# Interleaving the weight blocks in pairs, and walking the moving tiles of the rounded products from the last token to the first

## The chip, the cores and the metric

The kernel runs on one core of a Trainium2 chip. The metric is the device time in microseconds (us) of one execution. The median of three runs of the kernel before is 1629.67 us (1629.29 to 1630.35).

## The reference

Two transformer-like blocks are applied to 512 tokens of width 1024, all in float32. The first block normalises, projects with `w_in`, runs three mixers (a gated delta rule, a sparse attention with a learned index, a convolution), projects back with `w_out`, adds a cross-attention to a memory of 256 tokens, and ends with a two-layer network of width 4096. The second block projects with a matrix to seven times the width (`w_in_2`), runs a gated convolution and a gated linear recurrence, merges the two through four more projections, and ends with a gated network of width 2816.

```python
x = x + jnp.square(jax.nn.relu(rms_norm(x, norm_mlp) @ mlp_w1)) @ mlp_w2      # first block, its end
proj = rmsnorm(x, ln1_g) @ w_in                                               # second block
merged = sigmoid(gate_a + bias_0) * (y_a @ w_out_a) + sigmoid(gate_b + bias_1) * (y_b @ w_out_b)
x = x + merged @ w_o
x = x + (silu(h @ w_ffn_gate) * (h @ w_ffn_up)) @ w_ffn_down
```

Nearly all arithmetic is in these dense products of 512 tokens with weight matrices.

## The kernel before

Activations lie turned: 128 features on the partitions, the 512 tokens along the row. A tile is 128 features by 512 tokens. Each weight matrix is cut on the host into blocks of 128 by 128 (`panels`), and up to eight blocks that feed one output tile lie side by side as a panel of 128 x 1024 values. The SyncE queue brings 276 panels in order through two buffers `raw` (`sync_program`).

A dense product is computed in three products of rounded values. Each panel is split once into `w_hi`, the value rounded to the chip's rounded 32-bit type, and `w_lo`, what is left: ScalarE writes `w_hi` (L1384 in most of the kernel) and VectorE `w_lo` (L1981), into four slots of 1024 columns each. Activations are split alike, into `h_hi` and `h_lo`, `u_hi` and `u_lo`, and so on. For each block, `products` (L622 to L628) issues three matmuls into one accumulator of TensorE's memory: `w_hi` with the high activations, `w_hi` with the low ones, `w_lo` with the high ones. The weight block is the stationary operand, which is loaded anew for every matmul (one LDWEIGHTS each), the activation tile is the moving operand. `panel` (L630) walks the blocks of a panel; it first waits until the panel is split, and at its end it gives the slot back (`s_panel_used`). The order of the panels and of the products is written out by hand in `tensor_program`: the projection of the first block, whose products stand between the small matmuls of the delta rule as filler (`front`, `FILL`), then the cross-attention, then loops (`Fori`) over the two halves of the first network (up, down), the seven projections of the second block (`mix_tile`, panels of 7 or 8 blocks by `MIX_CUTS`), the merge, `w_o`, the gated network and its down projection (panels of 6, 6, 5 and 5 blocks by `DOWN_CUTS`).

Where operands lie in a partition of the on-chip memory is set in `plan_memory`: buffers follow each other from an aligned base, and L203 puts the activations at a fixed remainder. `w_hi` and `w_lo` begin at bytes that are 128 modulo 512, the activation buffers of the large stages at 192 modulo 512, and the pair `ub_hi`, `ub_lo` of the recurrence at 416.

```python
    top[0] += (192 - top[0]) % 512
    h0 = top[0]
    k.h_hi, _ = sb("h_hi", KT * T, F32R)
```

A block of 128 columns is 512 bytes of a partition, a moving tile 2048 bytes, so these remainders are the same for all blocks and tiles of a buffer.

Some matmuls are of other kinds. L692 multiplies the memory's values with the operands exchanged: activations `m_hi` and `m_lo` are stationary there and the weight panel is moving. L764, L800 and others work on unrounded values.

Of the kernel before, what the change touches and what calls it, by code (L numbers as in the profile page):

```python
# [54 lines left out]
WT_BANKS, GO_BANKS = (6, 7, 1, 2), (2, 0, 2, 0)  # L55
PAIRS, BEAT = TT * HEADS, 3

F32 = mybir.dt.float32
# [429 lines left out]


def til(buf, j, n=1, w=T):  # L490

    return buf[:, j * w:(j + n) * w]
# [122 lines left out]
def tensor_program(nc, k):  # L615
# [7 lines left out]

    def products(out, w_at, wn, a_hi, a_lo, first, last):

        for n, (w, a) in enumerate(((k.w_hi, a_hi), (k.w_hi, a_lo), (k.w_lo, a_hi))):
            mm = e.matmul(out, w[:, w_at:w_at + wn], a, start=first and n == 0, stop=last and n == 2)  # L627
        return mm  # L628

    def panel(out, hi, lo, tiles, first=True, last=True, at=0, done=True, w=T, ready=None):  # L630

        slot = pan.slot().start
        if at == 0:

            e.wait_ge(k.s_split_done, RAW + pan.at(1))
        for n, t in enumerate(tiles):
            if ready:
                e.wait_ge(ready[0], ready[1] + t + 1)  # L640
            mm = products(out, slot + (at + n) * P, P, hi[:, t * w:(t + 1) * w], lo[:, t * w:(t + 1) * w],
                          first and n == 0, last and n == len(tiles) - 1)
        if done:
            mm.then_inc(k.s_panel_used, 1)
            pan.step()
        return mm
# [419 lines left out]
    for j in range(0, KT, 2):  # L1066

        width = 2 if j == 0 else 1
        for j0 in range(j, j + 2, width):
            outs = [acc.take(e, 4 + (j0 + n) % 2) for n in range(width)]  # L1070
            slots = []
            for n in range(width):
                e.wait_ge(k.s_split_done, RAW + pan.at(1))
                slots.append(pan.slot().start)
                pan.step()
            for t in range(KT):
                if t < HEADS:
# [62 lines left out]
    def wo_part(tiles, heads):  # L1140

        for n in tiles:
            if heads[0] == 0:
                acc.take(e, n)
                if n % 2 == 0:
                    e.wait_ge(k.s_split_done, RAW + pan.at(1))
                    wo_slots.append(pan.slot().start)
                    pan.step()
            for h in heads:
                e.wait_ge(k.s_ao_lo_done, h + 1)  # L1150
                mm = products(k.ps[n][:], wo_slots[n // 2] + (HEADS * (n % 2) + h) * P, P, til(k.ao_hi, h), til(k.ao_lo, h),
                              h == 0, h == HEADS - 1)
            if h == HEADS - 1:
                mm.then_inc((k.s_wo_first, k.s_panel_used)[n % 2], 1)
# [48 lines left out]
    for a, b in ((0, 4), (4, 6), (6, 7), (7, KT)):  # L1203

        for n in range(2):
            if a == 0:
                acc.take(e, n)
                e.wait_ge(k.s_split_done, RAW + pan.at(1))
                up_slots.append(pan.slot().start)
                pan.step()  # L1210
            for t in range(a, b):
                e.wait_ge(k.s_fed_lo, 3 * KT + t + 1)
                mm = products(k.ps[n][:], up_slots[n] + t * P, P, til(k.h_hi, t), til(k.h_lo, t), t == 0, t == KT - 1)
            if b == KT:
                mm.then_inc(k.s_panel_used, 1)
                if n == 0:
                    sum_squares(4 * KT, 3, k.sqacc)
    for j in range(2, 4):
        panel(acc.take(e, j)[:], k.h_hi, k.h_lo, range(KT))
    for half in range(2):  # L1220

        with e.Fori(0, MTH // 4 - (half == 0)) as i:
            pan.enter(i, 4)
            acc.enter(i, [2, 2, 0, 0, 0, 0, 0, 0])
            for j in range(4):
                panel(acc.take(e, j % 2)[:], k.h_hi, k.h_lo, range(KT))
            pan.leave(MTH // 4 - (half == 0))
            acc.leave(MTH // 4 - (half == 0))
        with e.Fori(0, KT // 2) as i:
            pan.enter(i, 4)  # L1230
            acc.enter(i, [1, 1, 0, 0, 0, 0, 0, 0])
            for j in range(2):
                out = acc.take(e, j)[:]
                ready = (k.s_up_lo, MTH * half)
                panel(out, k.u_hi, k.u_lo, range(0, 8), last=False, ready=ready)
                panel(out, k.u_hi, k.u_lo, range(8, 16), first=False, ready=ready)
            pan.leave(KT // 2)
            acc.leave(KT // 2)
# [7 lines left out]
    def mix_tile(u_lo, opening):  # L1246

        for a, b in zip(MIX_CUTS, MIX_CUTS[1:]):
# [6 lines left out]
            for n in order:  # L1255
# [23 lines left out]
    for n, (hi, lo) in enumerate(both):  # L1279
# [3 lines left out]
        for t in range(KT - 1):  # L1283
            e.wait_ge(k.s_s2_free, t + 1)
            products(out[:], slots[n] + t * P, P, til(hi, t), til(lo, t), t == 0, False)
        pan.step()
    e.wait_ge(k.s_s2_free, KT)
    for n, (hi, lo) in enumerate(both):
        t = KT - 1
        products(k.ps[n][:], slots[n] + t * P, P, til(hi, t), til(lo, t), False, True).then_inc(k.s_panel_used, 1)  # L1290
    for n, (hi, lo) in enumerate(both):
        panel(acc.take(e, 2 + n)[:], hi, lo, range(KT))
    with e.Fori(0, KT // 2 - 1) as i:
        pan.enter(i, 4)
        acc.enter(i, [1, 1, 1, 1, 0, 0, 0, 0])
        for j in range(2):
            for n, (hi, lo) in enumerate(both):
                panel(acc.take(e, 2 * j + n)[:], hi, lo, range(KT))
        pan.leave(KT // 2 - 1)
# [3 lines left out]
    with e.Fori(0, 2) as i:  # L1303
        pan.enter(i, 4)
        acc.enter(i, [2, 2, 0, 0, 0, 0, 0, 0])
        for j in range(4):
            panel(acc.take(e, j % 2)[:], k.mg_hi, k.mg_lo, range(KT), ready=(k.s_mg_lo, 0))
        pan.leave(2)
# [3 lines left out]
    for j in range(4):  # L1312
        panel(acc.take(e, j)[:], k.h_hi, k.h_lo, range(KT), ready=(k.s_fed_lo, 5 * KT))
        if j == 0:
            sum_squares(6 * KT, 5, k.sqacc)
    with e.Fori(0, FFN // 2 - 1) as i:
        pan.enter(i, 4)
        acc.enter(i, [1, 1, 1, 1, 0, 0, 0, 0])
        for j in range(4):
            panel(acc.take(e, j)[:], k.h_hi, k.h_lo, range(KT))  # L1320
# [1412 lines left out]


# [71 lines left out]
```

## Time and profile before

| | |
|---|---|
| median of three runs | 1629.67 us |
| the profiled execution, first to last instruction | 1626.4 us |
| TensorE matmuls busy | 1595.6 us (98%), 7524 matmuls |
| TensorE weight loads busy | 1311.0 us (81%), 7524 loads |
| VectorE busy | 912.4 us (56%) |
| ScalarE busy | 684.1 us (42%) |
| GpSimd busy | 157.1 us (10%) |
| DMA | 149.50 MB, mean 92 GB/s |
| mean granted TensorE clock | 0.997 of full |

The profile's page gives no time of the profiled execution other than this span; the rest of this document works on the span. Matmuls overlap each other in the trace: a record lasts from its start to the modelled arrival of its last result. What one matmul costs in a stream is therefore the distance from its start to the next start, not its duration. `acc` is any of the eight accumulators, and numbers of buffers and tiles are left out of all names.

### The profile page before, as it was taken

How to read it: one execution, taken by the hardware profiler on the slowest of the kernel's cores; microseconds unless marked ns; L12 is line 12 of the kernel's file. 1: busy time of each engine (PE TensorE's matmuls, PEld its weight loads, DVE VectorE, ACT ScalarE, POOL GpSimd, SP SyncE). 2: the span in 40 equal slices, each digit the busy share in tenths (PEclk: the TensorE clock that was granted, in tenths of full speed). 3: DMA queues.
4: the chain of work that ended last, by engine and by line, in shares of the span. 5: the costliest groups of instructions: out<-in, count | busy, mean ns of one | idle time of the engine just before them, and what ended most of it. 6: DMA issues, size and time to landing. Idle time of an engine off the chain costs nothing.

```text
span 1626.4 us, 21588 instructions
## 1 busy us (share of the span) xinstructions
PE 1595.6 (98%) x7524; PEld 1311.0 (81%) x7524; DVE 912.4 (56%) x1319; ACT 684.1 (42%) x996; POOL 157.1 (10%) x97
## 2 busy tenths in 40 slices
PE   6999999999999999999999999999999999999997
PEld 5888798788788888888888888888888888888886
DVE  4549799765664323444377666666455544444332
ACT  5735554554653213433244545554224434443221
POOL 3445486100000000000000000000000000000000
PEclk9999999999999999999999999999999999999999
DMA  7521100122123232233233333333322323222332
GB/s 286 165 78 65 52 1 2 65 86 96 40 91 103 91 103 90 90 104 103 59 105 106 93 93 93 93 93 104 104 90 91 104 90 102 91 93 86 99 97 77
DMA packets 45665, 149.50 MB, mean 92 GB/s; under 512 B 4784, under 2 KB 5936, under 8 KB 45616
## 3 DMA queue, kind: packets, MB, share of 16 engines
q1 hardware_dynamic: 42240, 139.90, 27.1%
q10 hardware_dynamic: 3376, 8.95, 1.5%
q8 instruction: 31, 0.51, 0.1%
q14 instruction: 18, 0.15, 0.0%
HBM read 146.47 MB, written 2.10 MB: 91 GB/s over the span
## 4 chain that ended last, share of the span: by engine, by line
PE 91%; DVE 6%; DMA 1%; ACT 1%; issue 0%; ACTq 0%; DVEq 0%; SPq 0%
PE acc L627 84%; DVE c_acc L2105 1%; DVE tok L2243 1%; DMA x<-xT 1%; DVE d_score_a L2246 1%; PE acc L938 1%; DVE d_score_b L2246 1%; PE acc L963 1%; PE acc L1113 0%; PE acc L1134 0%; DVE g_x L2229 0%; PE acc L800 0%; PE acc L702 0%; DVE w_lo L1973 0%; DVE x L2681 0%
## 5 line engine op out<-in xcount | busy, mean ns | idle before, releaser
L627 PE MATMUL acc<-h_hi,w_hi 128*128 128x512 f32 x1248 | 492.3, 394 | 1.4 <-issue 0.8
L627 PE MATMUL acc<-h_hi,w_lo 128*128 128x512 f32 x1248 | 491.6, 394 | 0.0
L627 PE MATMUL acc<-h_lo,w_hi 128*128 128x512 f32 x1248 | 488.7, 392 | 0.0
L1981 DVE TENSOR_TENSOR w_lo<-raw,w_hi 128x1024 fp32r<-128x1024 f32 (+2 forms) x241 | 281.5, 1171 | 81.7 <-ACT w_hi L1384 59.7
L1384 ACT ACTIVATE w_hi<-raw 128x1024 fp32r<-128x1024 f32 (+2 forms) x241 | 241.9, 1007 | 178.2 <-PE acc L627 86.4
L627 PEld LDWEIGHTS acc<-h_hi,w_hi 128*128 128x128 f32 x1248 | 234.8, 188 | 54.3 <-issue 3.8
L627 PEld LDWEIGHTS acc<-h_lo,w_hi 128*128 128x128 f32 x1248 | 234.9, 188 | 53.4 <-issue 1.0
L627 PEld LDWEIGHTS acc<-h_hi,w_lo 128*128 128x128 f32 x1248 | 234.9, 188 | 49.2
L627 PE MATMUL acc<-u_hi,w_hi 128*128 128x512 f32 x256 | 100.9, 394 | 0.0
L627 PE MATMUL acc<-u_hi,w_lo 128*128 128x512 f32 x256 | 100.4, 392 | 0.0
L2384 DVE TENSOR_TENSOR x<-x,acc 128x512 f32 x32 | 22.0, 688 | 139.2 <-PE acc L627 138.7
L627 PE MATMUL acc<-u_lo,w_hi 128*128 128x512 f32 x256 | 99.3, 388 | 0.0
L2651 DVE TENSOR_TENSOR f_t<-acc,rstd 128x512 f32<-128x512 f32 x44 | 30.4, 691 | 98.5 <-PE acc L627 98.3
L627 PE MATMUL acc<-f_hi,w_lo 128*128 128x512 f32 x176 | 69.3, 394 | 0.0
L627 PE MATMUL acc<-f_lo,w_hi 128*128 128x512 f32 x176 | 69.0, 392 | 0.0
L553 POOL TENSOR_TENSOR w_lo<-raw,w_hi 128x1024 fp32r<-128x1024 f32 x25 | 61.3, 2452 | 78.5 <-ACT w_hi L1377 78.2
L627 PE MATMUL acc<-f_hi,w_hi 128*128 128x512 f32 x176 | 68.3, 388 | 0.0
L1911 ACT ACTIVATE f_hi<-f_t 128x512 f32 x22 | 13.9, 632 | 116.5 <-DVE f_t L2657 116.5
L1825 ACT ACTIVATE u_t<-u_t 128x512 f32<-128x512 f32 x32 | 20.2, 632 | 93.9 <-DVEq L2526 88.8
L2523 DVE SCALAR_TENSOR_TENSOR u_t<-acc,rstd 128x512 f32<-128x512 f32 x28 | 19.4, 691 | 69.1 <-PE acc L627 69.1
L627 PEld LDWEIGHTS acc<-u_hi,w_lo 128*128 128x128 f32 x256 | 48.1, 188 | 11.3
L627 PEld LDWEIGHTS acc<-u_lo,w_hi 128*128 128x128 f32 x256 | 48.1, 188 | 10.8
(394 smaller groups left out, 2323.1 us busy)
## 6 DMA issues: line engine op xcount, KB each, us to landing
raw<-panels_a SPq DMA_DIRECT2D x112, 512.0 KB, 3.3
raw<-panels_b SPq DMA_DIRECT2D x68, 512.0 KB, 3.3
raw<-mix SPq DMA_DIRECT2D x48, 448.0 KB, 3.4
raw<-mix SPq DMA_DIRECT2D x16, 512.0 KB, 3.7
raw<-down SPq DMA_DIRECT2D x16, 384.0 KB, 3.2
raw<-down SPq DMA_DIRECT2D x16, 320.0 KB, 2.9
x<-xT ACTq DMA_DIRECT2D x4, 1024.0 KB, 9.5
x_rows<-xN ACTq DMA_DIRECT2D x2, 1024.0 KB, 8.6
```

The lines of the kernel that those rows point to most:

```text
L553: TTn(lo, raw, hi.bitcast(F32), ALU.subtract).then_inc(k.s_split_done, 1)
L627: mm = e.matmul(out, w[:, w_at:w_at + wn], a, start=first and n == 0, stop=last and n == 2)
L938: e.matmul(k.ps[4 + u % 2][:, 0:(qt + 1) * P], k.d_q[r, (h // 2) * T + qt * P:(h // 2) * T + (qt + 1) * P], k.d_k[r, 0:(qt + 1) * P], star ...
L963: mm = e.matmul(k.ps[(7, 3)[qt % 2]][:, h * 64:(h + 1) * 64], k.d_pt[:, (u % 2) * T + t * P:(u % 2) * T + (t + 1) * P], k.d_v[:, t * 64:(t ...
L1384: A(k.w_hi[:, ahead.slot(w)], k.raw[:, ahead.unsplit(w)], ACT.Copy).then_inc(k.s_weights_hi, 1)
L1825: A(k.u_t[:, (2 + j % 2) * T:(3 + j % 2) * T], k.u_t[:, (j % 2) * T:(j % 2 + 1) * T], ACT.Square).then_inc(k.s_up_sq, 1)
L1981: TTn(lo, raw, k.w_hi[:, ahead.slot(w)].bitcast(F32), ALU.subtract).then_inc(k.s_split_done, 1)
L2105: ins = STT(out=out, in0=y, scalar=w, in1=out, op0=ALU.mult, op1=ALU.add)
L2246: replaced[qt] = link(e.match_replace(scores[qt], tok(TOK_M8 + 8 * qt - 8, 8), scores[qt], TAKEN))
L2384: TTn(x, x, k.ps[b][:], ALU.add).then_inc(k.acc_free[b], 1)
L2523: STT(out=til(k.u_t, j % 2), in0=k.ps[j % 2][:], scalar=0.0, in1=k.rstd[:], op0=ALU.max, op1=ALU.mult).then_inc(k.acc_free[j % 2], 1)
L2651: TTn(til(k.f_t, j + 2 * n), k.ps[b][:], k.rstd[:], ALU.mult).then_inc(k.acc_free[b], 1)
```

## The change

A stage is given a pair `(n, turned)` in a table `ORDER`, and every stage has `(2, True)`.

The first value is about the weights. On the host, `ordered` takes the blocks of a panel two by two and interleaves their columns: column 0 of the first block, column 0 of the second, column 1 of the first, and so on. In the kernel `stationary` picks a block out again by a view of every second column, so that its 128 columns are 8 bytes apart and spread over 1024 bytes. Where a panel has an odd number of blocks, its last block stays as it was, with columns side by side. The panels of the memory's values (`wv`), whose weights are the moving operand, stay as they were.

The second value is about the moving tile. `turned_back` gives it with its columns in descending order, and the output in descending order too, so that each token's result lands where it did.

Number, size and order of the instructions, transfers, waits and buffers stay the same; the split of a panel works on all its columns as before.

```diff
--- before.py
+++ after.py
+ORDER = {"front": (2, True), "up0": (2, True), "dn0": (2, True), "up1": (2, True), "dn1": (2, True), "mix": (2, True), "merge": (2, True), "w_o": (2, True), "ffn": (2, True), "down": (2, True)}
...
+def stationary(w, slot, block, blocks, order):
+
+    n, _ = order
+    g = block // n * n
+    n = min(n, blocks - g)
+    a = slot + g * P + block - g
+    return w[:, a:a + (P - 1) * n + 1:n]
+
+
+def turned_back(ap, order):
+
+    return ap[:, ::-1] if order[1] else ap
...
-    def products(out, w_at, wn, a_hi, a_lo, first, last):
+    def products(out, slot, block, a_hi, a_lo, first, last, order, blocks=KT):
 
         for n, (w, a) in enumerate(((k.w_hi, a_hi), (k.w_hi, a_lo), (k.w_lo, a_hi))):
-            mm = e.matmul(out, w[:, w_at:w_at + wn], a, start=first and n == 0, stop=last and n == 2)
+            mm = e.matmul(turned_back(out, order), stationary(w, slot, block, blocks, order), turned_back(a, order), start=first and n == 0, stop=last and n == 2)
...
-    def panel(out, hi, lo, tiles, first=True, last=True, at=0, done=True, w=T, ready=None):
+    def panel(out, hi, lo, tiles, first=True, last=True, at=0, done=True, w=T, ready=None, order=ORDER["front"], blocks=KT):
...
-            mm = products(out, slot + (at + n) * P, P, hi[:, t * w:(t + 1) * w], lo[:, t * w:(t + 1) * w],
-                          first and n == 0, last and n == len(tiles) - 1)
+            mm = products(out, slot, at + n, hi[:, t * w:(t + 1) * w], lo[:, t * w:(t + 1) * w],
+                          first and n == 0, last and n == len(tiles) - 1, order, blocks)
...
-                    mm = products(out[:], slot + t * P, P, til(k.y_hi, t), til(k.y_lo, t), t == 0, t == KT - 1)
+                    mm = products(out[:], slot, t, til(k.y_hi, t), til(k.y_lo, t), t == 0, t == KT - 1, ORDER["front"])
...
-        panel(acc.take(e, j)[:], k.h_hi, k.h_lo, range(KT))
+        panel(acc.take(e, j)[:], k.h_hi, k.h_lo, range(KT), order=ORDER["up0"])
...
-                mm = products(out[:], slot + (n - a) * P, P, til(hi, t), til(lo, t), first, last)
+                mm = products(out[:], slot, n - a, til(hi, t), til(lo, t), first, last, ORDER["mix"], b - a)
...
-                      ready=(k.s_f_lo_done, 0))
+                      ready=(k.s_f_lo_done, 0), order=ORDER["down"], blocks=b - a)
...
+def ordered(p, order):
+
+    n, _ = order
+    out, blocks = [], p.shape[2] // P
+    for g in range(0, blocks, n):
+        b = p[:, :, g * P:min(g + n, blocks) * P].reshape(p.shape[0], P, -1, P)
+        out.append(b.transpose(0, 1, 3, 2).reshape(p.shape[0], P, -1))
+    return out[0] if len(out) == 1 else np_concatenate(out)
...
-    panels_a = cat([wk, wv, panels(w_in), panels(a["w_out"][0]), panels(a["xa_wq"][0]), wo,
-                    up[:MTH], dn[0], up[MTH:], dn[1]], 0)
+    fr = lambda p: ordered(p, ORDER["front"])
+    panels_a = cat([fr(wk), wv, fr(panels(w_in)), fr(panels(a["w_out"][0])), fr(panels(a["xa_wq"][0])), fr(wo),
+                    ordered(up[:MTH], ORDER["up0"]), ordered(dn[0], ORDER["dn0"]), ordered(up[MTH:], ORDER["up1"]),
+                    ordered(dn[1], ORDER["dn1"])], 0)
...
+    mix = cat([ordered(mix[:, :, s * P:t * P], ORDER["mix"]) for s, t in zip(MIX_CUTS, MIX_CUTS[1:])], 2)
...
-    panels_b = cat([merge, panels(a["w_o_2"][0]), ffn], 0)
+    panels_b = cat([ordered(merge, ORDER["merge"]), ordered(panels(a["w_o_2"][0]), ORDER["w_o"]), ordered(ffn, ORDER["ffn"])], 0)
...
+    down = cat([ordered(down[:, :, s * P:t * P], ORDER["down"]) for s, t in zip(DOWN_CUTS, DOWN_CUTS[1:])], 2)
...
```

Every other call of `products` and `panel` for rounded products gets its stage's `order` in the same way.

## Rows read from the trace of the kernel before

**Rows 1.** The page: busy time, share of the span and instructions of each engine.
```profile
PE 1595.6 (98%) x7524; PEld 1311.0 (81%) x7524; DVE 912.4 (56%) x1319; ACT 684.1 (42%) x996; POOL 157.1 (10%) x97
```

**Rows 2.** The page: the chain that ended last, by engine and by line.
```profile
PE 91%; DVE 6%; DMA 1%; ACT 1%; issue 0%; ACTq 0%; DVEq 0%; SPq 0%
PE acc L627 84%; DVE c_acc L2105 1%; DVE tok L2243 1%; DMA x<-xT 1%; DVE d_score_a L2246 1%; PE acc L938 1%; DVE d_score_b L2246 1%; PE acc L963 1%; PE acc L1113 0%; PE acc L1134 0%; DVE g_x L2229 0%; PE acc L800 0%; PE acc L702 0%; DVE w_lo L1973 0%; DVE x L2681 0%
```

**Rows 3.** The same chain in order of time: shares, then start, length, what.
```profile
by line: PE acc L627 84.1%; DVE c_acc L2105 1.1%; DVE tok L2243 1.1%; DMA x<-xT 1.0%; DVE d_score_a L2246 0.7%; PE acc L938 0.6%; DVE d_score_b L2246 0.5%; PE acc L963 0.5%; issue 0.5%; PE acc L1113 0.5%; PE acc L1134 0.4%; DVE g_x L2229 0.
...
105.53 3.57 PE acc L764 x32
...
165.59 6.87 PE acc L800 x16
...
456.59 350.88 PE acc L627 x1533
809.09 3.36 DVE rstd L1964
813.81 442.07 PE acc L627 x1929
1256.74 357.09 PE acc L627 x1560
```

**Rows 4.** Busy time in three stretches: PE, PEld, DVE, ACT, POOL, clock, DMA.
```profile
456.00:807.00 351.00, 351.00 (x1534) 287.87 (x1533) 145.97 (x162) 113.78 (x144) 0.00 (x0) 1.00 0.30 96
813.00:1255.00 442.00, 441.35 (x1927) 361.81 (x1927) 285.83 (x361) 195.27 (x238) 0.00 (x0) 1.00 0.33 98
1257.00:1613.00 356.00, 356.00 (x1557) 292.08 (x1556) 152.00 (x177) 126.20 (x147) 0.00 (x0) 1.00 0.29 90
```

**Rows 5.** Instructions in order of time at 1300 us: start, length, what.
```profile
1300.30 0.39 PE L627 MATMUL acc<-h_hi,w_lo 128*128 128x512 f32 x1
1300.31 0.19 PEld L627 LDWEIGHTS acc<-h_hi,w_hi 128*128 128x128 f32 x1
1300.54 0.39 PE L627 MATMUL acc<-h_hi,w_hi 128*128 128x512 f32 x1
1300.54 0.19 PEld L627 LDWEIGHTS acc<-h_lo,w_hi 128*128 128x128 f32 x1
```

**Rows 6.** The same view, matmuls alone, of L692 at 27 us.
```profile
27.43 0.39 PE L692 MATMUL acc<-w_lo,m_hi 128*128 128x512 f32 x1
...
29.30 0.39 PE L692 MATMUL acc<-w_hi,m_hi 128*128 128x512 f32 x1
```

**Rows 7.** The same view, of the products with `ub` at 821 us.
```profile
821.48 0.40 PE L627 MATMUL acc<-ub_hi,w_hi 128*128 128x512 f32 x1
...
822.88 0.40 PE L627 MATMUL acc<-h_hi,w_hi 128*128 128x512 f32 x1
```

**Rows 8.** The same view, of the products with 256 tokens at 26 us.
```profile
25.79 0.28 PE L627 MATMUL acc<-m_hi,w_lo 128*128 128x256 f32 x1
...
26.50 0.28 PE L627 MATMUL acc<-m_hi,w_lo 128*128 128x256 f32 x1
```

**Rows 9.** Busy time of L627's instructions alone in a first stretch: PE, PEld, clock, DMA.
```profile
0.00:40.00 40.00, 14.57 (x96) 14.21 (x96) 1.00 0.77 286
```

**Rows 10.** Who PE waited for: total us, times, longest us.
```profile
PE acc L627 <- DVE w_lo L1973: 11.6, 1, 11.6
...
PE acc L627 <- DVE w_lo L1981: 0.7, 1, 0.7
```

**Rows 11.** The splits of panels, by line: count, duration min/median/max, forms.
```profile
L1981 DVE TENSOR_TENSOR w_lo<-raw,w_hi x241: 824/1224/1228, 344.7 to 1600.9; 128x1024 fp32r<-128x1024 f32 x90, 128x896 fp32r<-128x896 f32 x16, 128x640 fp32r<-128x640 f32 x8, 128x768 fp32r<-128x768 f32 x7
```

**Rows 12.** The same view of ScalarE's half of the split.
```profile
L1384 ACT ACTIVATE w_hi<-raw x241: 722/1045/1065, 340.1 to 1600.1; 128x1024 fp32r<-128x1024 f32 x90, 128x896 fp32r<-128x896 f32 x16, 128x640 fp32r<-128x640 f32 x8, 128x768 fp32r<-128x768 f32 x7
```

More of the change, by code:

```diff
@@ L1150, in wo_part @@
                 e.wait_ge(k.s_ao_lo_done, h + 1)
-                mm = products(k.ps[n][:], wo_slots[n // 2] + (HEADS * (n % 2) + h) * P, P, til(k.ao_hi, h), til(k.ao_lo, h),
-                              h == 0, h == HEADS - 1)
+                mm = products(k.ps[n][:], wo_slots[n // 2], HEADS * (n % 2) + h, til(k.ao_hi, h), til(k.ao_lo, h),
+                              h == 0, h == HEADS - 1, ORDER["front"])
             if h == HEADS - 1:
@@ L1212, in tensor_program @@
                 e.wait_ge(k.s_fed_lo, 3 * KT + t + 1)
-                mm = products(k.ps[n][:], up_slots[n] + t * P, P, til(k.h_hi, t), til(k.h_lo, t), t == 0, t == KT - 1)
+                mm = products(k.ps[n][:], up_slots[n], t, til(k.h_hi, t), til(k.h_lo, t), t == 0, t == KT - 1, ORDER["up0"])
             if b == KT:
@@ L1225, in tensor_program @@
             for j in range(4):
-                panel(acc.take(e, j % 2)[:], k.h_hi, k.h_lo, range(KT))
+                panel(acc.take(e, j % 2)[:], k.h_hi, k.h_lo, range(KT), order=ORDER[f"up{half}"])
             pan.leave(MTH // 4 - (half == 0))
@@ L1234, in tensor_program @@
                 ready = (k.s_up_lo, MTH * half)
-                panel(out, k.u_hi, k.u_lo, range(0, 8), last=False, ready=ready)
-                panel(out, k.u_hi, k.u_lo, range(8, 16), first=False, ready=ready)
+                panel(out, k.u_hi, k.u_lo, range(0, 8), last=False, ready=ready, order=ORDER[f"dn{half}"])
+                panel(out, k.u_hi, k.u_lo, range(8, 16), first=False, ready=ready, order=ORDER[f"dn{half}"])
             pan.leave(KT // 2)
@@ L1284, in tensor_program @@
             e.wait_ge(k.s_s2_free, t + 1)
-            products(out[:], slots[n] + t * P, P, til(hi, t), til(lo, t), t == 0, False)
+            products(out[:], slots[n], t, til(hi, t), til(lo, t), t == 0, False, ORDER["merge"])
         pan.step()
@@ L1289, in tensor_program @@
         t = KT - 1
-        products(k.ps[n][:], slots[n] + t * P, P, til(hi, t), til(lo, t), False, True).then_inc(k.s_panel_used, 1)
+        products(k.ps[n][:], slots[n], t, til(hi, t), til(lo, t), False, True, ORDER["merge"]).then_inc(k.s_panel_used, 1)
     for n, (hi, lo) in enumerate(both):
-        panel(acc.take(e, 2 + n)[:], hi, lo, range(KT))
+        panel(acc.take(e, 2 + n)[:], hi, lo, range(KT), order=ORDER["merge"])
     with e.Fori(0, KT // 2 - 1) as i:
@@ L1297, in tensor_program @@
             for n, (hi, lo) in enumerate(both):
-                panel(acc.take(e, 2 * j + n)[:], hi, lo, range(KT))
+                panel(acc.take(e, 2 * j + n)[:], hi, lo, range(KT), order=ORDER["merge"])
         pan.leave(KT // 2 - 1)
@@ L1306, in tensor_program @@
         for j in range(4):
-            panel(acc.take(e, j % 2)[:], k.mg_hi, k.mg_lo, range(KT), ready=(k.s_mg_lo, 0))
+            panel(acc.take(e, j % 2)[:], k.mg_hi, k.mg_lo, range(KT), ready=(k.s_mg_lo, 0), order=ORDER["w_o"])
         pan.leave(2)
@@ L1312, in tensor_program @@
     for j in range(4):
-        panel(acc.take(e, j)[:], k.h_hi, k.h_lo, range(KT), ready=(k.s_fed_lo, 5 * KT))
+        panel(acc.take(e, j)[:], k.h_hi, k.h_lo, range(KT), ready=(k.s_fed_lo, 5 * KT), order=ORDER["ffn"])
         if j == 0:
@@ L1319, in tensor_program @@
         for j in range(4):
-            panel(acc.take(e, j)[:], k.h_hi, k.h_lo, range(KT))
+            panel(acc.take(e, j)[:], k.h_hi, k.h_lo, range(KT), order=ORDER["ffn"])
         pan.leave(FFN // 2 - 1)
@@ L2732, in panels, with np_concatenate @@
     return w.reshape(kk // P, P, m // P, P).transpose(2, 1, 0, 3).reshape(m // P, P, kk)
+def ordered(p, order):
[5 more added lines that the diff above has]
+    return out[0] if len(out) == 1 else np_concatenate(out)
+def np_concatenate(parts):
+    import numpy as np
+    return np.concatenate(parts, 2)
 def kernel(**inputs):
```

## The prediction

> **What bounds the kernel now.** I read the page's busy line first [rows 1]: the reader sees that TensorE's matmuls cover 98% of the span, and no other engine more than 56%. A busy TensorE is not yet the bound, so the chain of waits comes next [rows 2]: 91% of it is on TensorE, and 84% on one line, L627, the three rounded products. The same chain in order of time [rows 3] shows how closed that is: from 456.59 us on there are three unbroken pieces of L627, of 1533, 1929 and 1560 products, and 350.88 / 1533 = 0.2289, 442.07 / 1929 = 0.2292 and 357.09 / 1560 = 0.2289 us per product. The table of busy time by stretch [rows 4] says why nothing else matters there: VectorE is busy 42%, 65% and 43% of the three stretches, ScalarE 32%, 44% and 35%, and the granted clock is 1.00, the level of 2.4 GHz. The list of waits has one long wait of TensorE for a split, 11.6 us at the start, and behind 456 us nearly none [rows 10]. So the time is (number of rounded products on the chain) x (distance between two starts), and the change can act only on the second factor: it leaves the number of instructions, the bytes and the waits alone.
>
> **How many products are on the chain.** 84.1% of 1626.4 us is 1368 us [rows 3]. About 13 us of that are the 96 products with 256 tokens, busy 14.57 us at the start [rows 9]. The other 1355 us at 0.2289 us are 5920 products of 512 tokens; 5022 of them are the three pieces [rows 3].
>
> **What a product costs beyond its columns.** 512 columns at 2.4 GHz are 213.3 ns. On the chain, 16 unrounded matmuls of the same shape at L800 took 6.87 us, 429.4 ns each [rows 3]; that is two passes of 213.3 and 2.7 ns over. Those too load their weights anew each time. Taking the same 2.7 ns for a rounded product, its floor is 216.0 ns, and its 228.9 ns hold a surplus of 12.9 ns, 5920 x 12.9 = 76.4 us in all. That is what the change plays for.
>
> Where the surplus comes from is an inference. The load of the next weights starts with the running matmul, both at 1300.54 [rows 5], so both read on-chip memory together. And the surplus depends on where the operands lie. In the large stages the moving tile begins 64 bytes behind the weights modulo 512, and the distance is 228.9 ns. In L692 the roles are exchanged, hence the remainders too, and eight distances take 1.87 us, 233.8 ns [rows 6]. For `ub`, 288 bytes behind, six take 1.40 us, 233.3 ns [rows 7]. Same shape, same clock, 4.4 to 4.9 ns more. I read this as the two reads meeting in the same part of memory at times.
>
> **The change, part by part.** *Columns of the weights 8 bytes apart.* How fast a load walks can be bounded from the small matmuls of L764, where loading is the longer part: 3.57 / 32 = 111.6 ns for each 128 columns [rows 3]. That is 512 bytes in 112 ns, 4.6 bytes per ns. The moving tile walks 2048 bytes in 213 ns, 9.6 bytes per ns, so today it overtakes the load. With every second column the load spans 1024 bytes in the same 112 ns, 9.1 bytes per ns: the speeds agree. *Descending tiles.* Then it depends on direction whether the two run side by side, 64 bytes apart, or against each other. No row shows from which end a load begins. If it begins at its last column, today's reads cross, and the descending tile goes along with it; if at its first, they went along before and cross now. Ends of the cost of both edits together: all surplus gone, -12.9 ns a product; below that nothing can go while 512 columns are streamed. Upwards, a price like that of the worse positions is +4.7 ns; the surplus doubled, because the load opens twice as many stretches of memory, is +12.9 ns; a moving tile read at half rate would be 429.4 - 228.9 = +200.5 ns. I take half of the surplus, -6.45 ns: the speeds match, which favours a fixed distance between the reads, but the direction is unknown, and the rows at other positions still carry a surplus. So -6.45 x 5920 = -38.2 us.
>
> *Smaller parts.* The unpaired last blocks of odd panels (6 of the 8 panels of each of 8 passes in `mix_tile`, 2 of 4 in each of 8 of the down projection, 64 blocks, 192 products) keep their weights side by side but turn their tiles; at 6.5 ns this is 1.2 us either way and stays in the range. If a load with a stride took twice as long, 223 ns, it would still hide below 228.9 ns and set a floor of about 223, half of the gain; for the 96 products of 256 tokens, now 0.71 / 6 = 118 ns [rows 8], it would add 105 ns each, 10 us at most, of which the waits of the first 40 us (L627 busy 14.57 of 40) hide most. The descending output costs nothing if its writes keep pace with the columns. Splits, transfers and waits stay as they were. Were TensorE 3% faster, a panel of 24 products would take 5.34 instead of 5.49 us, against 1.22 us of VectorE and 1.05 us of ScalarE for its split [rows 11, 12]; VectorE's 65% in the fullest stretch would become 67%, so no new wait follows, nor at 6%, where it would be 69%.
>
> **The sum.** 1626.4 - 38.2 = 1588.2 us of span. The median of the runs shown is 3.3 us above the span; with it 1591.5 us.
>
> **What the Trainium skill adds.** The distances show that rounded matmuls with loads beside them cost 12.9 ns more than the floor, and that the positions of operands matter [rows 3, 6, 7]. "TensorE: Matmul & The Clock Gate" (section "Step-by-step: what each phase is for") says that TensorE has two independent read ports, so that loading the next weights takes nothing from the running matmul. By that rule the edit of the weights would change nothing, a result of 1630 us; by the rows the reads do disturb each other. A second rule speaks against the change: "Advanced Engine Details and Errata", section "Memory Cachelines", says that a TensorE output that is not contiguous slows matmuls significantly, every two neighbours should be contiguous; and that on-chip reads need two hits in 16 bytes. Columns 8 bytes apart have just two. Whether a descending output counts as contiguous it doesn't say; no row here shows one. Read strictly, it leads to a rival in which the output is the slow side, priced below by the unrounded products' rate.
>
> **The rivals.** *The whole surplus goes.* The reads run side by side and never meet. For it: equal speeds, and 64 bytes between them. Against: it needs the right direction and no other cause of the surplus. 1626.4 - 76.4 + 3.3 = 1553.3 us.
>
> *Nothing changes.* The surplus belongs to switching weights at full rate, not to addresses, and the 4 to 5 ns of [rows 6, 7] to something else in those places. For it: all three long pieces have the same distance within 0.3 ns although their tiles lie in different buffers. Against: their remainders are equal, and where they differ the distance does. 1629.7 us.
>
> *The load disturbs more than before: slower.* Its 128 columns now touch twice as many stretches, or the tile meets it head-on; each meeting holds the moving tile for a beat. Place: every rounded product. Price: from +4.7 ns, the worse positions, to +12.9 ns, a doubled surplus: 5920 x 4.7 = 27.8 us, 1657.5 us; 5920 x 12.9 = 76.4, 1706.1 us. It decides from the point where the number of meetings, and not their length, makes the surplus. For it: twice the stretches is certain. Against: at its speed the load stays in each stretch for half as long, so that there are more meetings but shorter ones.
>
> *Descending operands stream at half rate,* the tile or the output. 5920 x 200.5 ns = 1187 us, some 2817 us. For it stands only that no row has a descending operand; the unrounded products show that such a rate exists [rows 3].
>
> **How the numbers follow.** Part of the surplus goes, forecast 1591.5 us: 0.38. The whole: 0.18. Nothing: 0.17. Slower by more meetings: 0.24. Half rate: 0.03. A comparison of this kernel tells 0.2%, 3.3 us, from no change. Faster 0.56, same 0.17, slower 0.27. The range reaches from the whole surplus, 1550, to just past the price of the worse positions, 1660; the doubled surplus (about 0.1) and the half rate stay outside. Since cases of both signs hold most of the chance, the likeliest one's own range stands beside it: 1570 to 1615.
>
> **What the profile of the changed kernel would show.** The three pieces of L627 should again be unbroken, with the same counts, and their length divided by them about 222 ns; 216 would be the second case, 229 the third, 234 to 242 the fourth, 430 the fifth. Within a stage, products on unpaired blocks would differ from their neighbours if the stride does the work, and be like them if the direction does. L692, which is not changed, should keep 234 ns. Matmuls of 256 tokens at 220 ns instead of 118 would say that a load with a stride takes twice as long. My forecast is wrong if the distance moves by less than 1 ns or grows, or if the gain shows elsewhere than in the distance, for instance if a wait for `w_lo` opens between panels.

## The result, and the profile after

The changed kernel takes 1656.67 us (median of four runs, 1655.27 to 1657.07), the kernel before 1629.48 us in the same comparison. The ratio is 1.0166, with a 95% interval of 1.0151 to 1.0180: it is slower by 27.2 us, clear of noise. The forecast of 1591.5 us had the wrong sign. The time is that of the rival in which the load disturbs more than before, at its lower price (1657.5 us), though the experiments below do not bear out its mechanism.

The page of the changed kernel comes first: busy time by engine, then the chain by engine. They answer to [rows 1] and the first line of [rows 2].

```profile
PE 1622.3 (98%) x7524; PEld 1354.6 (82%) x7524; DVE 910.7 (55%) x1319; ACT 683.2 (41%) x996; POOL 156.4 (9%) x97
...
PE 91%; DVE 6%; DMA 1%; ACT 1%; issue 0%; ACTq 0%; DVEq 0%; SPq 0%
```

The counts of TensorE's instructions and the shares of the chain are the same, and only TensorE's two sums grew: matmuls by 26.7 us, loads by 43.6 us. The other engines do the same work beside it. Now the chain of the changed kernel in order of time, for [rows 3]; the rounded products are at L642 there.

```profile
462.67 357.70 PE acc L642 x1533
821.99 3.36 DVE rstd L1979
826.70 450.38 PE acc L642 x1929
1277.94 364.01 PE acc L642 x1560
```

The three unbroken pieces have their old counts, 5022 products in all, and are 6.82, 8.31 and 6.92 us longer, together 22.05 us, or 4.39 ns a product. The first of them begins 6.08 us later; the some 900 products before it make 4.0 us of that at the same price. The remaining 2 us lie in that first part and are not traced further; among the kernels below whose products take the same 233.3 ns, this piece starts anywhere from 460.43 to 463.85 us. The span grew by 28.1 us in all.

357.70 / 1533 is 233.3 ns. In the order of time the intervals are even; this is the changed kernel, matmuls alone, at 1310 us (start, length, what).

```profile
1309.98 0.40 PE L642 MATMUL acc<-h_hi,w_hi 128*128 128x512 f32 x1
1310.21 0.40 PE L642 MATMUL acc<-h_lo,w_hi 128*128 128x512 f32 x1
1310.44 0.40 PE L642 MATMUL acc<-h_hi,w_lo 128*128 128x512 f32 x1
...
1311.38 0.40 PE L642 MATMUL acc<-h_hi,w_hi 128*128 128x512 f32 x1
```

The record of a weight load grew as well. These are loads between 1320 and 1330 us, with durations in ns as least, median and most: first the kernel before (L627), then the changed one (L642).

```profile
L627 PEld LDWEIGHTS acc<-h_hi,w_lo x15: 188/188/188, 1320.0 to 1329.6; 128*128 128x128 f32 x15
```

```profile
L642 PEld LDWEIGHTS acc<-h_hi,w_lo x15: 194/195/196, 1320.0 to 1329.8; 128*128 128x128 f32 x15
```

Finally the clock and the busy times of the changed kernel in nearly the stretches of [rows 4] (PE, PEld, DVE, ACT, POOL, clock, DMA share, GB/s), and the first waits of TensorE, for [rows 10].

```profile
462.00:816.00 354.00, 354.00 (x1517) 296.20 (x1516) 146.02 (x162) 113.56 (x144) 0.00 (x0) 1.00 0.29 95
826.00:1270.00 444.00, 443.43 (x1901) 370.20 (x1901) 282.81 (x357) 193.77 (x236) 0.00 (x0) 1.00 0.31 96
```

```profile
PE acc L642 <- DVE w_lo L1988: 11.6, 1, 11.6
PE acc L707 <- DVE w_lo L1988: 3.4, 4, 1.3
```

The granted clock is 1.00 in both kernels, TensorE is busy all but without a gap, and no wait was added in the large stages: behind 456 us its waits in either kernel are three of at most 0.7 us each. All of the loss there is in the distance between two starts.

### The profile page after: what moved, and what is told of

The parts are those of the page before. It is cut to its first block, busy times and chain, and to the rows that moved or that the text cites. A ratio compares the mean times of both kernels' runs of the same rounds, so it can differ in the third digit from the quotient of the medians.

```text
span 1654.5 us, 21588 instructions
## 1 busy us (share of the span) xinstructions
PE 1622.3 (98%) x7524; PEld 1354.6 (82%) x7524; DVE 910.7 (55%) x1319; ACT 683.2 (41%) x996; POOL 156.4 (9%) x97
## 4 chain that ended last, share of the span: by engine, by line
PE 91%; DVE 6%; DMA 1%; ACT 1%; issue 0%; ACTq 0%; DVEq 0%; SPq 0%
PE acc L642 84%; DVE c_acc L2120 1%; DVE tok L2258 1%; DMA x<-xT 1%; DVE d_score_a L2261 1%; PE acc L953 1%; DVE d_score_b L2261 1%; PE acc L978 0%; PE acc L1128 0%; PE acc L1149 0%; DVE g_x L2244 0%; PE acc L815 0%; PE acc L717 0%; DVE w_lo L1988 0%; DVE x L2696 0%
## 5 line engine op out<-in xcount | busy, mean ns | idle before, releaser
L642 PE MATMUL acc<-h_hi,w_hi 128*128 128x512 f32 x1248 | 502.3, 402 | 1.3 <-issue 0.8
L642 PE MATMUL acc<-h_lo,w_hi 128*128 128x512 f32 x1248 | 497.1, 398 | 0.0
L642 PE MATMUL acc<-h_hi,w_lo 128*128 128x512 f32 x1248 | 496.9, 398 | 0.0
L642 PEld LDWEIGHTS acc<-h_hi,w_hi 128*128 128x128 f32 x1248 | 244.0, 196 | 51.5 <-issue 3.8
L642 PEld LDWEIGHTS acc<-h_hi,w_lo 128*128 128x128 f32 x1248 | 244.1, 196 | 48.2
L642 PEld LDWEIGHTS acc<-h_lo,w_hi 128*128 128x128 f32 x1248 | 244.1, 196 | 47.4 <-issue 0.9
L642 PE MATMUL acc<-u_lo,w_hi 128*128 128x512 f32 x256 | 101.8, 398 | 0.0
L642 PE MATMUL acc<-u_hi,w_hi 128*128 128x512 f32 x256 | 101.8, 398 | 0.0
L642 PE MATMUL acc<-u_hi,w_lo 128*128 128x512 f32 x256 | 101.8, 398 | 0.0
L642 PE MATMUL acc<-f_hi,w_lo 128*128 128x512 f32 x176 | 70.0, 398 | 0.0
L642 PE MATMUL acc<-f_lo,w_hi 128*128 128x512 f32 x176 | 70.0, 397 | 0.0
L642 PE MATMUL acc<-f_hi,w_hi 128*128 128x512 f32 x176 | 69.9, 397 | 0.0
L642 PEld LDWEIGHTS acc<-u_hi,w_lo 128*128 128x128 f32 x256 | 50.0, 195 | 9.7
L642 PEld LDWEIGHTS acc<-u_hi,w_hi 128*128 128x128 f32 x256 | 50.0, 195 | 9.8
```

Source lines behind the costliest of these rows:

```text
L642: mm = e.matmul(turned_back(out, order), stationary(w, slot, block, blocks, order), turned_back(a, order), start=first and n == 0, stop=la ...
```

## The experiments

The distance is read from the first of the three long pieces of each kernel's chain (1533 products), except where the text says otherwise. "Remainder" is where the activation buffers begin, modulo 512 bytes; the weights are at 128 in all kernels. Kernels with one run carry no interval.

| load's columns | tile | remainder | ns a product | median, us | ratio to before |
|---|---|---|---|---|---|
| side by side (before) | ascends | 192 | 228.9 | 1629 to 1631 | 1 |
| pairs (the change) | descends, output too | 192 | 233.3 | 1656.67 | 1.0166 |
| pairs | ascends | 192 | 233.3 | 1656.26 | 1.0162 (1.0145 to 1.0179) |
| side by side | descends, output too | 192 | 233.3 | 1656.80 | 1.0162 (1.0145 to 1.0179) |
| side by side | descends, output ascends | 192 | 233.3 | 1657.47 | one run |
| side by side | ascends, output descends | 192 | 228.9 | 1627.93 | one run |
| fours | ascends | 192 | 239.9 | 1697.99 | 1.0413 (1.0396 to 1.0431) |
| side by side | descends, output too | 128 | 233.3 | 1656.06 | 1.0160 (1.0143 to 1.0177) |
| pairs | ascends | 128 | 233.3 | 1655.03 | 1.0162 (1.0145 to 1.0178) |
| one column repeated | ascends | 192 | 231.7 | 1644.98 | one run |
| one column repeated | descends, output too | 192 | 233.3 | 1654.39 | one run |
| one column repeated | ascends | 128 | 228.9 | 1633.02 | one run |
| side by side | one token repeated | 192 | 215.8 | 1556.80 | one run |
| side by side | ascends | 0 | 232.4 | 1650.81 | 1.0137 (1.0120 to 1.0154) |
| side by side | ascends | 64 | 233.3 | 1656.19 | 1.0163 (1.0146 to 1.0180) |
| side by side | ascends | 96 | 233.3 | 1655.45 | 1.0160 (1.0143 to 1.0177) |
| side by side | ascends | 128 | 226.7 | 1617.03 | 0.9921 (0.9904 to 0.9937) |
| side by side | ascends | 160 | 233.3 | 1654.69 | 1.0151 (1.0134 to 1.0168) |
| side by side | ascends | 256 | 233.3 | 1650.89 | one run |
| side by side | ascends | 384 | 226.7 | 1616.10 | 0.9913 (0.9897 to 0.9930) |

### Each edit alone

The changed kernel with one value of its table set back: pairs with ascending tiles, and turned tiles with weights side by side.

```diff
-ORDER = {"front": (2, True), ...
+ORDER = {"front": (2, False), ...
```

> The weights are interleaved in pairs, tiles and outputs ascend as before. Theory A (the load, its columns 8 bytes apart, opens twice as many stretches of memory and each costs the moving tile a beat): the distance between two rounded products is the 233.4 ns of the changed kernel or more, 1656 us or above. Theory B (what costs is the direction, tile and load now meet head-on): the distance stays at 228.9 ns or falls, at most 1630 us. Theory C (each edit has a share): about 231 ns, 1643 us.

```diff
-ORDER = {"front": (2, True), ...
+ORDER = {"front": (1, True), ...
```

> The weights lie side by side as before, tiles and outputs descend. Theory A (the stride costs): 228.9 ns a product, 1630 us. Theory B (the direction costs): 233.4 ns or more, 1656 us or above. Theory C (a share each): about 231 ns, 1643 us. If descending outputs or tiles were slow in themselves, it would be here, at far above 234 ns.

The first pieces of the two kernels' chains, pairs alone and then turned alone:

```profile
461.47 357.68 PE acc L642 x1533
```

```profile
463.49 357.70 PE acc L642 x1533
```

Both take 233.3 ns, as the two edits together do. Theory A had expected the second at 228.9 ns, theory B the first at most there, and theory C a share for each. Each edit costs the whole loss, and the other then costs nothing more. The load's record tells the edits apart where the time doesn't; these are again the loads at 1320 to 1330 us, of pairs alone and of turned alone.

```profile
L642 PEld LDWEIGHTS acc<-h_hi,w_lo x14: 194/194/198, 1320.5 to 1329.6; 128*128 128x128 f32 x14
```

```profile
L642 PEld LDWEIGHTS acc<-h_hi,w_lo x15: 187/188/188, 1320.1 to 1329.9; 128*128 128x128 f32 x15
```

The stride lengthens the record by 6 to 7 ns; descending tiles leave it alone, and cost the same.

The prediction had asked whether the products on unpaired blocks differ from the others. Such blocks stand in the second and third piece, not in the first. The third pieces, pairs alone and then turned alone:

```profile
1276.30 363.81 PE acc L642 x1560
```

```profile
1278.76 364.02 PE acc L642 x1560
```

With pairs alone the second piece is 0.41 us and the third 0.21 us shorter than with turned tiles alone, while the first is the same within 0.02 us. If the 192 products on unpaired blocks had kept the old distance, it would be 192 x 4.4 ns = 0.84 us (an estimate), so a good part of them seems to have kept it; they were not traced one by one. In the changed kernel the three pieces are as with turned tiles alone.

### A wider stride

```diff
-ORDER = {"front": (2, True), ...
+ORDER = {"front": (4, False), ...
```

> Blocks interleaved in fours, columns 16 bytes apart (12 in the last three blocks of a panel of 7), tiles ascending. Theory A (stretches opened count): twice as many again, so a further rise, by some 4.5 ns over the pairs if each stretch has a fixed price: 238 ns, 1683 us. Theory B (direction counts, the stride doesn't): as the pairs with ascending tiles. The record of a weight load was 188 ns before and 196 ns with pairs and descending tiles: if the stride makes that, it grows again here, and the direction does if it is 188 ns.

It took 1697.99 us. The first piece of its chain, and its loads at 1320 to 1330 us:

```profile
474.25 367.81 PE acc L642 x1533
```

```profile
L642 PEld LDWEIGHTS acc<-h_hi,w_lo x15: 309/315/315, 1319.7 to 1329.8; 128*128 128x128 f32 x15
```

239.9 ns are 6.6 ns over the pairs, more than the fixed 4.5 ns that theory A put on it, and the load's record jumps by 120 ns. A fixed price for each stretch opened doesn't describe 188, 195 and 315 ns. The products of 256 tokens, which have half the columns to stream and the same load, tell how long such a load keeps TensorE (same kernel, fours):

```profile
24.15 0.40 PE L642 MATMUL acc<-m_hi,w_lo 128*128 128x256 f32 x1
...
26.95 0.40 PE L642 MATMUL acc<-m_hi,w_lo 128*128 128x256 f32 x1
```

Twelve distances take 2.80 us, 233.3 ns each, against 118 ns before [rows 8]. So in fours the load alone accounts for all but 6.6 ns of the 239.9 ns, and this run does not tell whether a stride disturbs the moving tile more. That 233.3 ns is also the distance of the pairs may be chance; no run shows a link. A load with columns 16 bytes apart is a slower load; with 8 bytes it hardly is.

### Tile or output

Here the moving tile alone descends, then the output alone; the weights lie side by side in both. The tokens of each result come out in reverse order, so neither kernel computes the reference.

```diff
-            mm = e.matmul(turned_back(out, order), stationary(w, slot, block, blocks, order), turned_back(a, order), ...
+            mm = e.matmul(out, stationary(w, slot, block, blocks, order), turned_back(a, order), ...
```

> Weights side by side; only the moving tiles descend, the outputs ascend, so each rounded product lands with its tokens in reverse order: what this kernel computes is not the reference, only its time counts. Turning tiles and outputs together gave 233.3 ns a product. Theory B (the tile's reads against the load's): 233.3 ns again. Rival (the descending output is the slow side): 228.9 ns.

```diff
+            mm = e.matmul(turned_back(out, order), stationary(w, slot, block, blocks, order), a, ...
```

> The other half: only the outputs descend, the moving tiles ascend; the tokens of each rounded product are in reverse order here too. Theory B: 228.9 ns, since writing to the accumulators meets no read of the on-chip memory. Rival (the descending output is slow): 233.3 ns.

The first pieces, tile alone and then output alone:

```profile
463.85 357.70 PE acc L642 x1533
```

```profile
455.64 350.90 PE acc L642 x1533
```

The descending tile makes the whole 233.3 ns. The descending output is free, at 228.9 ns.

### Is the surplus the walking of the reads at all?

The load repeats one column, or the tile one token, with weights side by side and ascending tiles. These kernels leave out the rest of the weights or of the tokens, and only their time is read.

```diff
+            mm = e.matmul(out, w[:, slot + block * P:slot + block * P + 1].broadcast_to([P, P]), a, ...
```

> Tiles and outputs ascend, remainders as in the kernel before, but the load of each block repeats its first column 128 times, so the weights are wrong and only the time counts. The load is as long in columns but opens one stretch of 4 bytes instead of 512 bytes. If the surplus over 216 ns comes from the two reads meeting: nearly all of it goes, 216 to 218 ns, about 1555 us. If it comes from loading and switching as such: 13 ns of surplus remain, 226.7 to 228.9 ns. In between (a fixed share and a share from meetings): the fixed share is what is left here.

```diff
+            mm = e.matmul(out, stationary(w, slot, block, blocks, order), a[:, 0:1].broadcast_to([P, a.shape[1]]), ...
```

> Weights and remainders as in the kernel before, but each rounded product reads the first token of its tile 512 times; results are wrong, only the time counts. The tile's read now stands still while the load walks 512 bytes. Theory M (each passing of one read by the other holds the tile for about 6.7 ns; there are two or three of them today): fewer passings, 220 ns or less if the load passes the resting tile once. Rival S (13.3 ns, the surplus over 213.3 ns that is left at remainder 128, belong to switching weights): 226.7 ns at least.

The first pieces, one column and then one token:

```profile
459.43 355.14 PE acc L642 x1533
```

```profile
449.63 330.87 PE acc L642 x1533
```

A tile that stands still brings 215.8 ns, the floor of 216.0 ns that the prediction took from the unrounded matmuls [rows 3], and 72.6 us less in all. So loading and switching the weights cost nothing beyond it, and the rival in which the surplus belonged to the switch falls. A load that stands still brings 231.7 ns, more than before: the number of stretches that the load opens does not make the surplus. It arises where the moving tile of a rounded product walks. The unrounded products of L800 walk their tiles too and show only 2.7 ns over two passes [rows 3]; no run tells why they are spared.

Then the standing load again, once with descending tiles and once at remainder 128.

```diff
+            mm = e.matmul(turned_back(out, order), w[:, slot + block * P:slot + block * P + 1].broadcast_to([P, P]), turned_back(a, order), ...
```

> The load repeats the first column of each block and stands still (weights wrong, only the time counts); tiles and outputs descend, remainder 192. With ascending tiles this load gave 231.7 ns. If direction counts only between two walking reads, it is 231.7 ns again with intervals from 226 to 235. If a descending tile costs in itself, whatever the load does, it is the flat 233.3 ns of all runs with descending tiles.

```diff
-    top[0] += (192 - top[0]) % 512
+    top[0] += (128 - top[0]) % 512
```

> The load that stands still, tiles ascending, remainder 128. If position acts through where load and tile begin, another value than the 231.7 ns at 192, whose direction says whether 128 is a good remainder for a standing load too (226.7 ns). If position acts only between two walking reads, 231.7 ns again.

The first pieces, turned and then at remainder 128:

```profile
460.43 357.70 PE acc L642 x1533
```

```profile
456.52 350.89 PE acc L642 x1533
```

With descending tiles it is the flat 233.3 ns whatever the load does. With ascending ones the position matters even to a load that stands: 231.7 ns at 192 and 228.9 ns in this piece at 128. The second piece at 128 is an exception that no run explains; it takes 231.2 ns a product:

```profile
813.74 446.08 PE acc L642 x1929
```

### The position

The kernel before with other remainders, and both edits at the best of them. The edit is always that of L203, here at 128:

```diff
-    top[0] += (192 - top[0]) % 512
+    top[0] += (128 - top[0]) % 512
```

> The kernel before with its activation buffers at 128 modulo 512 instead of 192, so that weights and tiles begin at the same remainder. If the surplus over 216 ns depends on where the two reads stand to each other, the distance leaves 228.9 ns, by the 4 to 5 ns of the two other positions in the profile of before or more: 233 ns, 1655 us. If the surplus belongs to something else (switching weights at full rate), 228.9 ns and 1630 us stay.

The first piece of its chain:

```profile
454.72 347.53 PE acc L627 x1533
```

347.53 / 1533 = 226.7 ns, with no instruction changed, and 1617.03 us. Position decides, and the direction of the effect was not the one that the expectation named.

> Weights side by side, tiles and outputs descend, activation buffers at 128 modulo 512. With ascending tiles this remainder took 2.2 ns off each product (226.7 instead of 228.9). In the kernel with descending tiles the products with ub, at another remainder, had the same 233.3 ns as the rest: if reads that run against each other meet equally often wherever they begin, it stays at 233.3 ns and 1657 us. If position matters there too: it moves by some ns, down to 226.7 ns and 1617 us at best.

> Weights interleaved in pairs, tiles and outputs ascending, activation buffers at 128 modulo 512. With the pairs at remainder 192 a product took 233.2 ns, with intervals from 230 to 236. If load and tile walk the same way at nearly the same speed, the distance between them stays, so the remainder should decide strongly: 220 ns or below, or 240 ns, and not 233. If the stride costs a fixed amount, 233 ns less the 2.2 ns that this remainder gives without stride: 231 ns, 1643 us.

The first pieces at remainder 128, turned alone and then pairs alone:

```profile
462.30 357.70 PE acc L642 x1533
```

```profile
461.24 357.67 PE acc L642 x1533
```

Neither edit gets anything from the better position: 233.3 ns, as at 192. For ascending pairs that refutes the idea behind the forecast, that with equal speeds the distance between the reads stays and so decides strongly. Descending pairs have two positions on record, both in the changed kernel: the large stages at 192, and `ub` at 416, whose six distances from 834.52 to 835.92 us are 233.3 ns each as well.

> The kernel before with its activations at 64 modulo 512, 64 bytes before the weights. Remainder 192 gave 228.9 ns, 128 gave 226.7 ns. Theory M: the number of passings is 2 or 3 for each product, so between 226.7 and 233.3 ns, 1617 to 1657 us. If 226.7 ns is one step on a slope towards fewer passings, below 226.7 ns.

> The kernel before with its activations at 0 modulo 512, 128 bytes before the weights. Theory M: between 226.7 and 233.3 ns as at 64. A value outside these two would say that more than the count of two or three passings is at work.

The first pieces, 64 and then 0:

```profile
463.09 357.69 PE acc L627 x1533
```

```profile
460.26 356.23 PE acc L627 x1533
```

> The kernel before with its activations at 256 modulo 512. If the pattern of memory that the two reads meet in repeats every 256 bytes, it is as at 0: 232.4 ns with single intervals of 241. If it repeats every 512 bytes or later, another value, between 226.7 and 233.3 ns.

> The kernel before with its activations at 384 modulo 512. If the pattern repeats every 256 bytes, the 226.7 ns and 1617 us of remainder 128. If not, 228.9 to 233.3 ns, and 128 is good because the tile begins at the weights' own remainder.

The first and third pieces at 256, then the first at 384:

```profile
460.59 357.70 PE acc L627 x1533
...
1274.03 362.52 PE acc L627 x1560
```

```profile
455.79 347.53 PE acc L627 x1533
```

384 agrees with 128 to the last digit of this piece. At 256 the third piece is the 362.52 us of remainder 0 (232.4 ns), but the first is 1.5 us longer than there. So the positions repeat every 256 bytes, in one stage with a small difference that no run explains.

> The kernel before with its activations at 160 modulo 512, half way between 128 (226.7 ns) and 192 (228.9 ns). If the distance changes smoothly with the position: near 227.8 ns, 1623 us. If 226.7 ns is only reached where load and tile begin at the same remainder: 229 ns or more. A lower value than 226.7 ns would be a better version.

> The kernel before with its activations at 96 modulo 512, 32 bytes before the weights. At 160, 32 bytes behind them, a product took 233 ns, at 128 226.7 ns, at 192 228.9 ns, so the dependence isn't smooth. If it is the same on both sides of 128, 233 ns and 1655 us; 64 bytes before and behind differ already (233.3 against 228.9 ns), so a value below 226.7 ns and below 1616 us isn't excluded.

The first pieces, 160 and then 96:

```profile
460.63 357.68 PE acc L627 x1533
```

```profile
461.55 357.69 PE acc L627 x1533
```

32 bytes to either side of 128, the distance is 233.3 ns. At 144, 16 bytes behind the weights, there is no result, since the buffers of this kernel can only begin at multiples of 32 bytes; what a smaller step does stays open. With the kernel's own walk, four of the positions tried are at or within 1 ns below it (64, 96, 160 and 0 with 256), and only 192 and 128 with 384 are clearly better.

All these kernels move the activations and leave the weights at 128. Whether the tile's own address counts, or where it begins relative to the stationary operand, can be read from L692, which has the same code in all of them and the roles exchanged: its moving tile is a weight panel that always begins at 128, and the stationary operand, `m_hi` or `m_lo`, begins at the remainder. In the kernel before it takes 233.8 ns [rows 6], or 233.3 ns over all its four groups of ten distances. With the activations at 64, the moving tile begins 64 bytes behind the stationary operand, as the large stages do at 192:

```profile
28.86 0.39 PE L692 MATMUL acc<-w_lo,m_hi 128*128 128x512 f32 x1
...
31.15 0.40 PE L692 MATMUL acc<-w_hi,m_lo 128*128 128x512 f32 x1
```

Ten distances take 2.29 us, 229 ns, and the four groups 229.5 ns. The moving tile has not moved; only the stationary operand has. Over the four groups L692 takes 232.3 ns at 0 and at 256, 233.3 ns at 160 and at 96, and 229.5 to 229.8 ns at 128 and 384. At 192 its tile begins 64 bytes ahead, and it takes what the large stages take at 64. So where the tile begins relative to the stationary operand decides, in the large stages and in L692. `ub`, 288 bytes behind its weights, fits too: that is one repeat of 256 bytes and 32 more, and it has the 233.3 ns of 160 [rows 7]. The sizes agree within 0.6 ns except at equal remainders, where L692 takes 3 ns more than the 226.7 ns of the large stages.

## Why the prediction was wrong

*The bound, the count and the floor* were right. The three pieces kept their counts, the loss is in the distance alone, and 4.39 ns x 5920 is 26.0 us of the measured 27.2. The floor of 216.0 ns was measured at 215.8.

*That the surplus comes from where and how the operands are read* was right, and is shown by the remainders and by the tile that stands still. "TensorE: Matmul & The Clock Gate" of the Trainium skill (section "Step-by-step: what each phase is for") lets loads of the next weights take nothing from a running matmul; the distances disagree where the tile of a rounded product walks, since 226.7 to 233.3 ns were measured where its rule leads to 216, and in L692 a move of the stationary operand alone, from 192 to 64, took the distance from 233.3 to 229.5 ns.

*The step that failed* is "I take half of the surplus, -6.45 ns: the speeds match, which favours a fixed distance between the reads". The term is +4.39 ns. I had weighed the change against the floor, as if 228.9 ns were what a product costs in an ordinary place. The runs show an ordinary level of 233.3 ns, which many unlike kernels share: descending tiles at two remainders and beside three kinds of load, pairs at two remainders, and the unchanged walk at remainders 64, 96 and 160. The remainder 192 of the kernel before is one of the few positions with relief, 4.4 ns below that level. Descending tiles lose the relief, and paired columns lose it. That is why each edit alone costs all of it, both together no more, and neither gains at remainder 128, where the relief is 6.7 ns. The premise of matching speeds had no row behind it either. It took L764's 111.6 ns for the time of a load, but a quarter of the 429.4 ns of L800, which has four times the columns, is 107.4 ns, so streaming alone fills nearly all of it (an estimate). And at either position tried, paired columns gave no gain. The prediction had the sign of this in its rows, since L692 and `ub` stood at 233.8 and 233.3 ns [rows 6, 7]; it read them as the worse positions, and they were the usual ones.

*The rival of more meetings* had the right size by its lower price, which came from the same two rows. Its mechanism is not borne out. For the tile, neither a head-on course nor the number of stretches is needed: beside a load that stands still, a descending tile has the same 233.3 ns. For the pairs, twice the stretches cost 4.4 ns at 192 but 6.6 ns at 128, and end at the level that unpaired weights have at 64. That the size fitted is in part luck.

*The smaller parts.* The descending output costs nothing, which settles the half-rate rival for both operands. The Trainium skill, "Advanced Engine Details and Errata", section "Memory Cachelines", wants outputs contiguous, and on-chip reads with two hits in 16 bytes. On the first the trace says: a descending output doesn't count as one that isn't contiguous, at 228.9 ns. The two hits bear on the load: with two, its record is 195 ns, with one, in fours, 315 ns. That a load with a stride could take twice as long was a false fear for pairs, and comes true in fours. L692, or L707 in the changed kernel, kept its 233.3 ns over four groups, as was expected of it. This is the changed kernel at 25 us, where six products of 256 tokens take 0.70 us, 117 ns each, after 118 ns before [rows 8].

```profile
25.58 0.28 PE L642 MATMUL acc<-m_hi,w_lo 128*128 128x256 f32 x1
...
26.28 0.28 PE L642 MATMUL acc<-m_hi,w_lo 128*128 128x256 f32 x1
```

*What stays open* is what in the memory gives the relief at some relations of the two starts, and why descending tiles and paired columns, whose load is hardly longer, lose it. From which end a load reads its columns no run shows; a load in the other direction wasn't tried. The repeat of 256 bytes is measured, its cause is not.

## What to carry to other kernels

Before an access pattern is changed in a kernel bound by streams of matmuls, measure what its present placement gives: the distance between starts at a few other start addresses shows whether the kernel stands on an ordinary level or on a favoured one, which the new pattern would give up. Here one number in the memory plan is worth more than both edits: with the activations at 128 modulo 512 instead of 192, the unchanged products take 226.7 ns, and the kernel 1617.03 us (ratio 0.9921, 0.9904 to 0.9937), the best version found together with its like at 384 (1616.10 us). The start to vary is that of one operand relative to the other. Two edits should be run apart even where both are meant for one effect, since their losses need not add.

## What the runs showed of the hardware that was not expected

- The distance of two rounded products of 512 columns is 233.3 ns in the first piece of eleven of the twenty kernels in the table, whatever was changed, 20 ns over the 213.3 ns of the columns. At the two best remainders it is 226.7 ns, 13.3 ns over, and with a tile that stands still 215.8 ns.
- A step of 32 bytes in where the tile begins, from 128 to 160 or to 96, moves the kernel from 1617 to 1655 us. What counts is the start of the tile relative to the stationary operand: in L692 the distance went from 233.3 to 229.5 ns with the tile in place and the stationary operand moved from 192 to 64.
- A moving tile in descending order takes 233.3 ns at every position tried, 192, 128 and `ub`'s 416. A descending output is free.
- The record of a load of 128 columns of 4 bytes is 188 ns side by side, 195 ns at 8 bytes apart, and 309 to 315 ns at 16 bytes apart. In products of 256 columns the last kind costs 233.3 ns a product, the pairs 117 ns.
